# Ada tiles in groups of four between groups of four weight tiles

## The reference

```python
def adaln(cond, w, b):                       # w: (2048, 6 * 2048)
    m = jax.nn.silu(cond) @ w + b
    return [t[:, None, :] for t in jnp.split(m, 6, axis=-1)]

for layer in range(2):
    shm, scm, gm, shf, scf, gf = adaln(cond, w_ada[layer], b_ada[layer])
    h = rmsnorm(y, g_pre_mix[layer]) * (1 + scm) + shm
    o = attention(h, w_att_in, w_att_out) if layer % 2 == 0 else recurrent(h, w_rec_in, w_rec_out)
    y = y + gm * rmsnorm(o, g_post_mix[layer])
    h = rmsnorm(y, g_pre_ffn[layer]) * (1 + scf) + shf
    y = y + gf * rmsnorm(relu(h @ w_ff1[layer]) ** 2 @ w_ff2[layer], g_post_ffn[layer])
```

## Time and profile before

| | |
|---|---|
| device time, median of 2 runs | 2500.1 us (2500.01 to 2500.18) |
| device time of the profiled execution | 2500.55 us |
| its span | 2498.8 us |
| mean granted TensorE clock | 0.97 of full speed |
| TensorE, VectorE, ScalarE busy | 94%, 60%, 44% of the span |
| moved by DMA | 593.10 MB, 237 GB/s over the span |

### The profile page before, as it was taken

The page is one execution under the profiler, slowest core; times in us unless marked ns, Lnnn a source line. Parts: engine busy times, 40 slices in busy tenths (PEclk is TensorE's granted clock), DMA queues, the critical chain, the costliest instruction groups (busy, mean ns, idle before and its releaser), DMA issues.

```text
span 2498.8 us, 29539 instructions
## 1 busy us (share of the span) xinstructions
PE 2354.5 (94%) x12179; PEld 1820.9 (73%) x12179; DVE 1492.1 (60%) x2055; ACT 1107.7 (44%) x1529; POOL 85.7 (3%) x139
## 2 busy tenths in 40 slices
PE   5799996989999999999998999897999999999996
PEld 1366666668888887777876777665888888778775
DVE  2344445456555556666667678865655556666665
ACT  0133334344333334555554358733444444555553
POOL 1000000000000000000000011000000000000000
PEclk8699998989999999999999999998999999999998
DMA  9989890765777777675674887687455655766763
GB/s 354 326 301 323 311 318 11 269 236 186 252 253 253 253 253 257 223 252 207 224 253 155 308 284 257 242 288 273 152 191 185 197 186 175 258 228 213 250 220 117
DMA packets 296405, 593.10 MB, mean 237 GB/s; under 512 B 11568, under 2 KB 11824, under 8 KB 296016
## 3 DMA queue, kind: packets, MB, share of 16 engines
q1 hardware_dynamic: 289744, 574.77, 66.0%
q0 software_dynamic: 6528, 16.46, 2.0%
HBM read 587.76 MB, written 3.42 MB: 237 GB/s over the span
## 4 chain that ended last, share of the span: by engine, by line
PE 87%; DMA 5%; DVE 4%; ACT 2%; issue 1%; POOL 1%; SPq 0%; DVEq 0%; ACTq 0%; POOLq 0%
PE bank L539 22%; PE bank L529 15%; PE bank L531 14%; PE bank L530 14%; PE bank L541 11%; PE bank L494 6%; DMA raw<-in_w_ada 4%; PE bank L646 2%; PE bank L556 1%; DVE w_lo L1029 1%; PE bank L680 1%; DVE x L1156 1%; DMA raw<-in_w_att_in 1%; POOL small L405 0%; ACT R L929 0%
## 5 line engine op out<-in xcount | busy, mean ns | idle before, releaser
L1029 DVE TENSOR_TENSOR w_lo<-raw,w_hi 128x1024 fp32r<-128x1024 f32 x712 | 858.0, 1221 | 519.5 <-ACT w_hi L778 517.5
L778 ACT ACTIVATE w_hi<-raw 128x1024 fp32r<-128x1024 f32 x712 | 734.2, 1051 | 727.5 <-DMA raw<-in_w_att_in 222.5
L539 PE MATMUL bank<-xt,w_hi 128*128 128x512 f32 x2560 | 907.2, 398 | 1.9 <-DVE R L1049 1.5
L541 PE MATMUL bank<-xt,w_lo 128*128 128x256 f32 x2560 | 716.3, 280 | 0.0
L529 PE MATMUL bank<-w_hi,xt 128*128 128x512 f32 x1568 | 623.9, 398 | 9.6 <-DVE w_lo L1029 4.3
L531 PE MATMUL bank<-w_hi,xt 128*128 128x512 f32 x1568 | 612.1, 390 | 0.0
L530 PE MATMUL bank<-w_lo,xt 128*128 128x512 f32 x1568 | 611.6, 390 | 0.0
L539 PEld LDWEIGHTS bank<-xt,w_hi 128*128 128x128 f32 x2560 | 479.9, 187 | 154.1 <-issue 38.6
L541 PEld LDWEIGHTS bank<-xt,w_lo 128*128 128x128 f32 x2560 | 483.2, 189 | 0.4
L529 PEld LDWEIGHTS bank<-w_hi,xt 128*128 128x128 f32 x1568 | 295.1, 188 | 146.0 <-issue 61.5
L531 PEld LDWEIGHTS bank<-w_hi,xt 128*128 128x128 f32 x1568 | 295.0, 188 | 63.1
(11 more groups left out here) (171 smaller groups left out, 913.1 us busy)
## 6 DMA issues: line engine op xcount, KB each, us to landing
raw<-in_w_ff SPq DMA_DIRECT2D x256, 1024.0 KB, 5.4
raw<-in_w_ada SPq DMA_DIRECT2D x192, 1024.0 KB, 5.6
raw<-in_w_att_in SPq DMA_DIRECT2D x36, 1024.0 KB, 7.4
raw<-in_w_rec_in SPq DMA_DIRECT2D x32, 1024.0 KB, 7.5
raw<-in_w_att_out SPq DMA_DIRECT2D x16, 1024.0 KB, 7.5
raw<-in_w_rec_out SPq DMA_DIRECT2D x16, 1024.0 KB, 7.6
gain_rows<-in_g_post_mix POOLq DMA_DIRECT2D x8, 256.0 KB, 4.5
gain_rows<-in_g_post_ffn POOLq DMA_DIRECT2D x8, 256.0 KB, 4.2
```

What stands on the lines that cost most here:

```text
L539: nc.tensor.matmul(ps[m][:, :], w_hi[:, h, k, m * P:(m + 1) * P], xt[:, c, :], start=(begin and k == 0), stop=False)
L541: mm = nc.tensor.matmul(ps[m][:, 0:NG * T], w_lo[:, h, k, m * P:(m + 1) * P], xt[:, c, 0:NG * T], start=False, stop=(end and k == 1))
L778: nc.scalar.activation(w_hi[:, h % NSPLIT, :, :], raw[:, slot, 2 * q:2 * q + 2, :], ACT.Copy)\
L1029: V.tensor_tensor(w_lo[:, h % NSPLIT, :, :], raw[:, slot, 2 * q:2 * q + 2, :], w_hi[:, h % NSPLIT, :, :].bitcast(fp32), ALU.subtract).then ...
```

## The change

Only the order strings change. The same tiles are read and multiplied, in the same slots by position, and every sweep keeps the length of its string.

```diff
-    ma = "MA" * 4
+    ma = "MMMMAAAA"
...
-        Sweep("ff1_0", 8, "feature", w["ff1_0"], 0, 4, 2, "cols", (1, 0), "MMA" * 4, "hidden"),
-        Sweep("ff2_0", 4, "token", w["ff2_0"], 0, 16, 1, "gate", (0, 20), "MMA" * 4 + "M" * 8, "op", False),
+        Sweep("ff1_0", 8, "feature", w["ff1_0"], 0, 4, 2, "cols", (1, 0), "MMMMAAAAMMMM", "hidden"),
+        Sweep("ff2_0", 4, "token", w["ff2_0"], 0, 16, 1, "gate", (0, 20), "MMMMAAAA" + "M" * 12, "op", False),
...
-        Sweep("ff2_1", 4, "token", w["ff2_1"], 0, 16, 1, "gate", (1, 20), "MMA" * 4 + "M" * 8, "op", False),
+        Sweep("ff2_1", 4, "token", w["ff2_1"], 0, 16, 1, "gate", (1, 20), "MMMMAAAA" + "M" * 12, "op", False),
```

## The result

The changed kernel takes 2792.83 us (median of 2 runs, 2791.55 to 2794.11) against 2500.10 (2500.01 to 2500.18): 1.117 times as long, 95% interval 1.1145 to 1.1199. The forecast was 2766, between 2695 and 2830. The span of the profiled execution is 2792.3 us, 293.5 more than before, and the mean granted clock 0.921 instead of 0.970.

A forecast was written before the change was run, and what follows sets the result against it. The prediction took TensorE's stream to bound the kernel. Per-boundary holes, less 0.96 us of saved switching and, inside stages, plus 1.7 of low clock, with stage ends and early ada tiles, added 265 us to 2500.1: 2766 us, range 2695 to 2830.

The forecast's parts named there:

- The slot: At group starts: the next first weight tile's load can't issue before TensorE finishes the first ada tile; three remain.
- Term 1: In TensorE's runs of four ada tiles: fewer switches save 0.96 us per run, 38 us over 40 runs.
- Term 2: After each run TensorE waits for load and splits: 5.0 us in token stages, up to 7.3 in rec_in_b.
- Stage ends: At the ends of att_in_b, rec_in_b and rec_out: 5.9 us more waiting each.
- Term 3: After each of the 37 holes inside stages: TensorE's clock is low for a while, costing 1.7 us each.
- Small terms: In ff1_0 and rec_in_a: three ada tiles formerly taken early, during the norm wait, now add 3 us.
- Rival 1: At SP's wait before a group's first weight tile: holes are covered and the run pays, 2462 us; chance 0.03.
- rival 2: In the holes after runs: they open but the clock falls in few or none, 2703 us; chance 0.17.
- rival 3: Holes cost more, by longer low clock, slower loads or VectorE and ScalarE falling behind: 2800 to 2865 us; chance 0.14.

The follow-up runs named there:

- alternating: Changed kernel with transfers still MMMMAAAA, but TensorE taking the eight tiles as M A M A M A M A: 2600.65 us, 1.0392 of the kernel before.
- late order: Changed kernel with transfers still MMMMAAAA, but TensorE taking the tiles as M M A M A M A A: 2522.12 us, 1.0094 of the kernel before.
- Banks first: Changed kernel, but ScalarE and VectorE take out the four banks ahead of the next split where a feature block follows a run: 2768.36 us.
- filled hole: Changed kernel with 20 useless identity matmuls after each run of ada tiles that a weight tile follows: 2736.72 us, 1.0942 of the kernel before.
- pairs: Changed kernel with order strings MMAA instead of MMMMAAAA, so runs of two: 2502.31 us, 1.0011 of the kernel before.
- threes: Changed kernel with order strings MMMAMAAA, a run of three ada tiles: 2639.33 us, 1.0557 of the kernel before.
- the two with cover: Changed kernel, transfers MMMMAAAA, TensorE taking M M A M A M A A in one and M M M A A M A A in the other: 2522.12 and 2534.03 us.

## Why the prediction was right

The direction, the mechanism and most of the sum held; the time came 27 us above the forecast, inside the range. No large errors cancel: the terms came out at about their forecast or above it. By the steps of the prediction:

- **The slot** (what the change does to the loads): right. SP issues the next M at 308.96, at the end of the first ada tile, and the experiments that moved the release alone moved the hole. That grouped transfers cost next to nothing by themselves is shown in ff1_0 by the alternating order of TensorE.
- **Term 1**, 0.96 saved per run: the run takes 3.64 us against 3.67 by its parts. One switch is worth 0.33 by the late order (0.32 forecast).
- **Term 2**, the holes: 5.0 forecast and 5.0 measured in token stages, 6.1 and 6.3 in ff2, 6.5 and 6.7 in ff1_0, 7.3 and 7.6 in rec_in_b; 222 us in all where the same terms add up to 219 (rec_in_a: 6.5 forecast, 6.3 measured). The landing took 5.1 us where the estimate from the Trainium skill, DMA: Bandwidth & Descriptors, section on the anatomy of one DMA, was 4.4: the row of the old trace was the better price. Banks first showed that the extra time in feature stages is the order of ScalarE and VectorE.
- **Stage ends**, 5.9: 8.03 - 2.11 = 5.9 at att_in_b. From TensorE's timeline, 9.30 instead of 2.69 at rec_in_b (6.6) and 9.01 instead of 2.16 at rec_out (6.9). What the prediction did not list is the entry into rec_out, where the fourth weight tile, the first that is not split ahead, waited 4.32 us for its split instead of 1.63, and its matmuls then ran at the low pitch.
- **Term 3**, the clock: right in kind (a filled hole loses under 0.2 us) and undersized: 80 / 37 = 2.2 us per hole where 1.7 was charged, 80 - 63 = 17 of the 27 us. The one old hole was half as long, and its 1.7 lies inside the new spread of 1.45 to 2.86.
- **Small terms**, 3: the waits for the norms of ff1_0 and rec_in_a are now 12.28 us both; in the old kernel they were 11.29 after one early ada tile and 10.43 after two. So these tiles no longer fill that wait, which costs 2.8 us.

The sum as measured: holes 222, clock 80, ends 19, early ada tiles 3, less 40 x 0.96 = 38, and less 4 for the one hole of the old kernel and its low pitch, which the new holes contain: 282 of 293.5. The entry of rec_out adds 2.7 us of waiting and about 2.3 of low pitch, and rec_in_b about 2.6: three waits of 1.3 us for a split, behind the turned ada row, where the old kernel had two of 0.7 behind the gates. Some 4 us stay open.

Rival 1 (no hole) and rival 2 (the clock stays up) fell with the first look at the timeline. Of rival 3, a smaller form of the longer low clock is what happened. What failed were my expectations for experiments: five of the eight times fell outside their ranges (pairs by 2 us, threes, alternating, and the two with cover by 12 and 29), and a sixth came short of its number (80 us of clock expected, 56 measured). For threes and alternating, and in rec_in_b for the late order, the timelines give one reason: I followed each slot by itself and not the order of the one queue that fills them all.

## What to carry to other kernels

In a ring of slots that one in-order queue fills, look for the slot whose release comes last, and ask what is queued behind it: every later load starts then at the earliest, free slot or not. A reordering that saves a third of a microsecond per switch pays only if the work left after the last release covers a load and all that stands between landing and first use, here 7.5 to 9 us. Where a hole can't be avoided, an engine whose clock falls when idle pays for it a second time.

## What the runs showed of the hardware

A 1 MB load issued when no other of these was under way took 5.1 us to land (median of 239); of the other 308 the median was 7.2 us.

Holes of the same length did not cost the same in clock: after 4.93 us (to 282.49) the low pitch cost 2.84 us, after 4.96 us (to 316.44) 1.45. In the run with the filled holes, remainders of 2.08 to 2.11 us in ff1_0 lost about 1.4 us at two boundaries and next to nothing at a third, and remainders of up to 1.7 us in token stages and ff2 lost under 0.2. In att_in_b, with useless matmuls in every hole, the granted clock was 1.00 (252 to 375 us) where it was 0.91 without them.
